# Softmax attentions of a two-block kernel: TensorE issues the scores of a pair three turns ahead of its transposes instead of two

## What is computed

```
# first block: 8 heads of 64, chunks of 64 tokens see themselves and the 8 chunks before
q, k = rmsnorm(q, q_norm_w), rmsnorm(k, k_norm_w)
scores = q k^T / 8 + rel_bias[clip(distance)]      # masked to the band of 9 chunks
y = softmax(scores) v

# second block: 16 query heads of 64 on 4 key heads, a window of 128 keys to either side
logits = q k^T / 8 - slope * |distance|            # masked to the window
m = max(logits.max(), sink);  p = exp(logits - m)
o = p v / (p.sum() + exp(sink - m))
```

## Time and profile before

| what | value |
|---|---|
| three timed runs | 2979.94, 2991.75, 2992.13 us; median 2991.75 us |
| profiled execution, its own time | 2978.78 us |
| its span in the profile | 2977.0 us |
| busy over the span: TensorE matmul, VectorE, GpSimd, ScalarE | 93%, 56%, 41%, 28% |
| first softmax attention | 262.2 to 314.6 us, 16 pairs |
| second softmax attention | 1085.8 to 1179.6 us, 32 pairs |

### The profile page before, as it was taken

How to read it: one execution, slowest core, us unless ns; L and a number is a source line. 1 busy time by engine, 2 the same in 40 slices (tenths; PEclk the granted TensorE clock), 3 DMA queues, 4 the chain that set the end, 5 groups by cost and what they waited for, 6 DMA issues and landing times.

```text
span 2977.0 us, 39216 instructions
## 1 busy us (share of the span) xinstructions
PE 2778.0 (93%) x13452; PEld 2234.1 (75%) x13452; DVE 1673.6 (56%) x3277; ACT 840.9 (28%) x1285; POOL 1212.9 (41%) x996
## 2 busy tenths in 40 slices
PE   6997899999999887999979879999999999999997
PEld 5855778878788665778767768888888888888775
DVE  4135541111699447579999964444444454454787
ACT  1143223322222436123444412222222222222111
POOL 4410255556454420544423234444444444444442
PEclk9998899999999999999999999999999999999998
DMA  4210023333232220222245564434434434434442
GB/s 141 86 36 22 22 92 99 93 93 103 85 93 92 77 79 30 83 83 78 85 177 204 219 176 115 134 106 120 127 106 123 125 108 124 126 109 123 120 131 66
DMA packets 207080, 313.39 MB, mean 105 GB/s; under 512 B 139792, under 2 KB 142224, under 8 KB 202768
## 3 DMA queue, kind: packets, MB, share of 16 engines
q1 hardware_dynamic: 63792, 233.39, 25.2%
q10 hardware_dynamic: 143200, 78.85, 9.5%
HBM read 274.45 MB, written 37.75 MB: 105 GB/s over the span
## 4 chain that ended last, share of the span: by engine, by line
PE 49%; issue 22%; POOL 14%; DVE 13%; ACT 1%; DVEq 0%; DMA 0%; POOLq 0%; ACTq 0%
PE bank L1205 15%; PE bank L1206 15%; PE bank L1207 15%; POOL lo L420 14%; PE bank L1524 1%; DVE bank L1158 1%; DVE ohg L1142 1%; DVE WH L1160 1%; DVE eq L1115 1%; DVE idx L1057 1%; DVE scb L1050 1%; DVE idx L1049 1%; DVE oh L1138 1%; DVE pr L831 1%; DVE oh L1139 0%
## 5 line engine op out<-in xcount | busy, mean ns | idle before, releaser
L420 POOL TENSOR_TENSOR lo<-raw,hi 128x256 fp32r<-128x256 f32 (+1 forms) x992 | 1212.7, 1249 | 1725.9 <-ACT hi L442 1059.5
L1205 PE MATMUL bank<-inH,hi 128*128 128x512 f32 x2240 | 889.7, 397 | 25.1 <-DVE inL L768 15.6
L1206 PE MATMUL bank<-inL,hi 128*128 128x512 f32 x2240 | 880.5, 393 | 0.0
L1207 PE MATMUL bank<-inH,lo 128*128 128x512 f32 x2240 | 878.6, 392 | 0.0
L1166 DVE TENSOR_TENSOR xT<-xT,bank 128x512 f32<-128x512 f32 x504 | 341.4, 688 | 550.9 <-PE bank L1207 550.9
L1205 PEld LDWEIGHTS bank<-inH,hi 128*128 128x128 f32 x2240 | 425.8, 190 | 118.2 <-issue 27.3
L1207 PEld LDWEIGHTS bank<-inH,lo 128*128 128x128 f32 x2240 | 425.6, 190 | 90.5
L1206 PEld LDWEIGHTS bank<-inL,hi 128*128 128x128 f32 x2240 | 426.0, 190 | 89.5 <-issue 2.2
L1205 PE MATMUL bank<-WH,hi 128*128 128x512 f32 x1024 | 406.5, 397 | 27.1 <-DVE WL L1161 14.6
L1206 PE MATMUL bank<-WL,hi 128*128 128x512 f32 x1024 | 404.3, 395 | 0.0
L1207 PE MATMUL bank<-WH,lo 128*128 128x512 f32 x1024 | 404.3, 395 | 0.0
(11 more groups left out here) (201 smaller groups left out, 2388.4 us busy)
## 6 DMA issues: line engine op xcount, KB each, us to landing
raw<-stream SPq DMA_DIRECT2D x440, 512.0 KB, 3.6
Gd<-gates ACTq DMA_DIRECT2D x32, 1024.0 KB, 7.3
gates<-stage_a ACTq DMA_DIRECT2D x16, 1024.0 KB, 3.9
gates<-stage_b ACTq DMA_DIRECT2D x16, 1024.0 KB, 4.0
tbl<-gqa ACTq DMA_DIRECT2D x8, 384.0 KB, 3.9
xT<-x SPq DMA_DIRECT2D x1, 2048.0 KB, 9.5
spilled<-res ACTq DMA_DIRECT2D x8, 256.0 KB, 3.8
A<-spilled ACTq DMA_DIRECT2D x4, 512.0 KB, 3.9
```

Source lines behind the costliest of these rows:

```text
L420: ins = pool.tensor_tensor(lo[:, r, part], raw[:, r, part], hi[:, r, part].bitcast(F32), ALU.subtract)
L1205: pe.matmul(bank, wh, xh, start=start, stop=False)
L1206: pe.matmul(bank, wh, xl, start=False, stop=False)
L1207: return pe.matmul(bank, wl, xh, start=False, stop=stop_)
```

## The change

TensorE's loop in the attention routine starts one turn earlier and issues in turn p the scores of pair p+1, ahead of T(p-2) and M(p-3). The order is now S(p+1), T(p-2), M(p-3). What is awaited ahead of a given S is the same as before: S of pair q waits for L of pair q-2, the last user of its two banks. No other engine's stream changes, and no instruction is added or removed.

```diff
             def attention(st):
                 s, pairs = st["s"], st["pairs"]
                 n = len(pairs)
-                for p in range(n + 3):
-                    if p < n:
-                        w = pairs[p]
-                        if p >= 2:
-
-                            pe.wait_ge(s["logit"], 2 * p - 2)
+                for p in range(-1, n + 3):
+                    if p + 1 < n:
+                        w, b = pairs[p + 1], (p + 1) % 2
+                        if p >= 1:
+
+                            pe.wait_ge(s["logit"], 2 * p)
                         for half in (0, 1):
-                            m = pe.matmul(B[SCORES[p % 2][half]][:, :w["n"]], st["qk"][ROWS[half], w["q"], w["i"] * P:(w["i"] + 1) * P],
+                            m = pe.matmul(B[SCORES[b][half]][:, :w["n"]], st["qk"][ROWS[half], w["q"], w["i"] * P:(w["i"] + 1) * P],
                                           st["qk"][ROWS[half], w["k"], w["k0"]:w["k0"] + w["n"]], start=True, stop=True)
                         m.then_inc(s["score"], 1)
                     v = p - 2
```

## The result

| | before | changed |
|---|---|---|
| timed runs, beside one another | 2979.94 to 2992.13, median 2983.86 us (6) | 2952.78 to 2960.34, median 2956.56 us (6) |
| span of the profiled execution | 2977.0 us | 2953.3 us |
| first attention, first to last start on L480 | 42.8 us | 36.8 us |
| second attention, the same | 85.7 us | 69.2 us |

The ratio is 0.9901, with a 95% interval of 0.9887 to 0.9915: 1.0% faster, 27.3 us by the medians and 23.7 us by the profiled spans. Forecast were 24.2 us and a time of 2967.5 us. Run again in another session, the change gave 2954.78 us against 2989.48 us, ratio 0.9894 (0.9875 to 0.9912).

A forecast was written before the change was run, and what follows sets the result against it. Both attentions were taken as bound by a ring of waits, no engine being full. Gains of 17.0 (second) and 7.2 us (first) sum to 24.2, off the median 2991.75: 2967.5 us, range 2952 to 2982.5.

The forecast's parts named there:

- The ring: Waits through L, E, C, T, M, S in both attentions: 5.70 us a round, moving two pairs before, three after.
- The second attention at VectorE's pace: VectorE's own work, 2.20 us a pair, sets the second attention: 68.2 us against 85.23, gain 17.0 us.
- The first attention: TensorE's 8.54 us a group plus 0.76 of remaining wait: 9.30 a group, 34.9 us against 42.07, gain 7.2 us.
- the walk: Three engine streams followed turn by turn in the first attention: 0.76 us a group remains of a 2.27 us copy wait.
- The new waits: VectorE waits 7.0 us for transposes in the first attention; its waits for scores fall from 30.1 us to under 3.
- The copies' waits: TensorE's transposes wait for copies 11.2 and 19.2 us in the two attentions; these shrink to some 6 us in each.
- The wait that S brings: On TensorE, scores wait for a more recent VectorE step, with transposes behind: price 0, at worst 0.85 us a turn.
- Rival 3: Scores stand in the way of transposes on TensorE in both attentions: 35.5 us slower, 3027 us; chance 0.04.
- Rival 4: Both attentions run at a low granted clock, TensorE 1.7 times slower: 40 us slower, 3031 us; chance 0.02.
- the rule on transposes: Skill's statement that transposes do not count as busy or run at full clock, putting a transpose-rich stage at risk; unpriced.

The follow-up runs named there:

- the lead of one: Scores stand one turn ahead of their pair's transposes in both attentions, where the kernel before has two: 3166.38 us against 2988.32, one execution.
- the copy first: Copy of transposes put ahead of the exponential on ScalarE: in the kernel before 2954.41 us (ratio 0.9896), in the changed kernel 2949.24 us (0.9884).
- The padding: Three small VectorE operations added per pair in the second attention: kernel before 2992.48 us (ratio 1.0022), changed kernel 2976.36 us (0.9971).
- the first attention alone: Kernel before with scores three turns ahead of their transposes in the first attention only, two in the second: 2974.18 us against 2988.32, ratio 0.9952.
- a lead of three: The changed kernel itself: scores three turns ahead of their pair's transposes, where the kernel before has two; median 2956.56 us, ratio 0.9901.
- a lead of four: Scores four turns ahead of their pair's transposes in both attentions, against two in the kernel before: 2975.55 us against 2988.32, ratio 0.9955.

## Why the prediction was right, and where it was off

*The ring.* Right. Its prices were read from seven starts in the earlier trace rows. That one round moves as many pairs as the lead has turns is borne out by the lead of one, and that any link would do by the copy first.

*The second attention at VectorE's pace.* Forecast 68.2 us from first to last exponential; measured 1152.34 - 1083.70 = 68.64. The gain was 16.6 us for a forecast of 17.0. Taking TensorE's work from starts rather than from shown durations decided this: 8.54 us a group is below VectorE's 8.80, where 9.40 would have been above. The padding confirms that VectorE bounds it.

*The first attention.* Forecast 34.9 us; measured 301.43 - 265.43 = 36.0, gain 6.1 us for 7.2. The wait kept ahead of T was put at 0.76 us a group where 2.27 stood; the walk behind that figure is not shown, but the changed kernel has it. The transposes of the third pair of a group:

```profile
272.46 1.54 PE L1319 MATMUL bank<-cs,pr 128*128 128x128 f32 x6 [0.91 <-ACT pT L492]
...
284.80 0.87 PE L1319 MATMUL bank<-cs,pr 128*128 128x128 f32 x6 [0.77 <-ACT pT L492]
...
294.17 0.87 PE L1319 MATMUL bank<-cs,pr 128*128 128x128 f32 x6 [0.77 <-ACT pT L492]
```

From 284.80 to 294.17, at the full clock, a group takes 9.37 us for a forecast of 9.30. From 272.46 to 284.80 it takes 12.34, 3.0 more. The difference is the clock, which the walk left at full speed. From 270 to 278 us it was granted at 0.63, and there VectorE waited 2.97 us for one set of transposes:

```profile
276.57 1.97 PE L1319 MATMUL bank<-cs,pr 128*128 128x128 f32 x8
...
278.68 0.56 DVE L831 CUSTOM_DVE_ANT_0 pr<-bank,tbl1b 128x384 f32<-128x384 f32 x1 [2.97 <-PE bank L1319]
```

The same x8 took 1.09 us at full clock. The kernel with the first attention alone bears this out: the same streams, a clock of 0.95 from first to last exponential instead of 0.91, and 35.2 us instead of 36.8. That the total is only 1.1 us above the forecast is partly luck: some 2 us were made up at the start and the end, where the sum took 9.30 us a group as everywhere.

*The new waits.* Forecast 7.0 us for transposes; measured 7.8, of which 2.97 are the one wait at the low clock, so the size agrees in part by luck. For scores under 3 us; measured 1.3. The copies' waits were to fall to some 6 us in each attention; they are 6.0 and 5.8.

*The wait that S brings.* Price 0 at a lead of three was forecast; there are 0.7 + 1.3 us of idle time on TensorE, and no run shows how much of it reached the time. Rival 3 was wrong here but right in kind: scores that wait ahead of ready transposes do close a ring at a lead of four, L, S, T, L and not rival 3's through C, and it costs 12.9 us in the second attention.

*Rival 4 and the rule on transposes.* In the changed kernel the second attention ran at a granted clock of 1.00 throughout, with transposes in every turn; before it was 0.98. The rule that transposes do not run at the full clock (the Trainium skill, TensorE: Matmul & The Clock Gate, PE-mode transpose) is contradicted by this trace too: six take 0.87 us at 284.80 and 1.54 at 272.46, so they speed up with the granted clock. Whether transposes count as busy, as the same sentence denies, stays open: here other matmuls always stand between them. The half of rival 4 that is true is that a starved TensorE falls to the low level: 0.57 at a lead of one.

*The time itself.* The sum of the terms was 24.2 us, and the profiled spans differ by 23.7. The predicted 2967.5 was 10.9 us too high because of one step: I set the gain against the median of the three runs shown and so assumed that the changed kernel's runs would lie as far above its profile as those. They do not: 2952.8 to 2960.3 with a span of 2953.3. Against the profiled execution, 2978.78 - 24.2 = 2954.6 would have been 2.0 us off. What lay above it goes with the clock. The 33 executions of the kernel before in the sessions of the experiments have mean granted clocks from 0.964 to 0.972, and their times fall from 2994.0 to 2978.6 us as the clock rises; the profiled execution has 0.972. The ten executions of the changed kernel have 0.970 to 0.973. The forecast had no term for that, and it is also why the medians differ by more than the spans: at 0.971 the two kernels are 24.3 us apart (the estimate above), which the sum of 24.2 meets. Why the kernel before more often falls to the lower clock stays open.

## What to carry to other kernels

Where several engines are each three quarters busy in a stage, look for the ring of waits in the timeline, divide its length by the number of items that one round moves, and compare with the fullest engine's own work per item: that is what can be gained, and it can be gained at any link (one more item in flight, or a link taken out). Give an in-order stream just the lead that it needs: one turn more put a wait for fresh work ahead of work that was ready, and lost more than half of the gain. Count an engine's work from start to start before moving work onto it; a small operation moved off the full engine bought nothing, since its new engine had no room.

## What the runs showed of the hardware

The granted clock followed how the ring was fed, by the same instructions: in the second attention 0.57 at a lead of one, where TensorE stood idle for 3.4 us in each round, and 1.00 at a lead of three. Before the low stretch in the first attention of the changed kernel (272 to 279 us) TensorE had been busy for 5.02 of the 8 us from 262 to 270; with the copy first as well it had been busy for 6.13 of them, and the clock stayed at 1.00 to the end of the attention. This is one comparison and no rule.

Stretches that no kernel was meant to change differed by several us between profiled executions of different kernels ("between" 780.5 to 784.2 us over the leads of two to four, the start 263.6 to 268.6). Their length went with the time that they spent at the lower clock: 30.7 us of it in the start of 263.6 us, 44.4 in that of 268.6; 47.8 to 58.0 us of it in "between" over these kernels. Two profiled executions of the changed kernel in different sessions had the low stretches in the same places (781.5 and 781.7 us; 265.4 and 265.6), but the program alone does not settle it, as the clocks of 0.964 to 0.972 of the kernel before show.
